# First attention of a two-block network: values' high and low parts in one tile, product by pairs of heads, halves added by VectorE

## What is computed

```python
dots  = einsum("bthd,bsd->bths", iq, ik)            # indexer
score = einsum("bth,bths->bts", iw, relu(dots))     # then causal
_, idx = lax.top_k(score, 256)                      # keys that a token may see
logits = einsum("bthd,btkd->bhtk", q, k_sel) * 64 ** -0.5 + bias
p = softmax(where(valid, logits, -inf))
o = einsum("bhtk,btkd->bthd", p, v_sel)
y_b = attn @ w_branch_b                             # merged with the convolution's y_a
```

## Time and profile before

| | |
|---|---|
| runs of the kernel | median 2590.57 us of 3 (2590.13 to 2590.76) |
| span of the profiled execution | 2590.4 us |
| PE busy | 2485.7 us (96%) |
| DVE, ACT, POOL busy | 1683.1, 950.8, 658.6 us |
| chain that ended last, by engine | PE 85%, DVE 8%, ACT 3% |
| the first attention's pipeline | about 497 to 650 us of the span |

### The profile page before, as it was taken

The page is one execution under the profiler, slowest core; times in us unless marked ns, Lnnn a source line. Parts: engine busy times, 40 slices in busy tenths (PEclk is TensorE's granted clock), DMA queues, the critical chain, the costliest instruction groups (busy, mean ns, idle before and its releaser), DMA issues.

```text
span 2590.4 us, 32111 instructions
## 1 busy us (share of the span) xinstructions
PE 2485.7 (96%) x12208; PEld 2054.2 (79%) x12208; DVE 1683.1 (65%) x2874; ACT 950.8 (37%) x1766; POOL 658.6 (25%) x536
## 2 busy tenths in 40 slices
PE   7899999988999999999999998999999999999998
PEld 5688888777787788888888886888877787888987
DVE  4599999477425898888654449585687556004843
ACT  5521212487224332222312144332333236226842
POOL 3157421576542100000000130000000035334753
PEclk9999999899999999999999999999999999999999
DMA  5112333100544365664533141323237223542242
GB/s 188 33 42 66 98 98 98 41 1 20 175 167 128 107 192 179 197 185 139 188 117 134 37 143 57 106 86 102 98 131 267 82 72 127 175 134 91 103 162 99
DMA packets 264324, 302.11 MB, mean 117 GB/s; under 512 B 11272, under 2 KB 216556, under 8 KB 264172
## 3 DMA queue, kind: packets, MB, share of 16 engines
q1 hardware_dynamic: 263860, 299.96, 35.6%
q10 hardware_dynamic: 312, 0.09, 0.0%
HBM read 228.15 MB, written 70.29 MB: 115 GB/s over the span
## 4 chain that ended last, share of the span: by engine, by line
PE 85%; DVE 8%; ACT 3%; issue 1%; DMA 1%; POOL 1%; SPq 0%; DVEq 0%; ACTq 0%; POOLq 0%
PE ps L67 82%; PE ps L70 3%; DVE sm L79 1%; DVE tmp L76 1%; ACT tmp L73 1%; ACT pth L73 1%; DVE pwa L76 1%; DVE wl L76 1%; DVE B2l L76 1%; DVE tmp L79 0%; DVE ptl L79 0%; DVE X L79 0%; ACT wh L73 0%; DVE pwb L76 0%; DVE XO L79 0%
## 5 line engine op out<-in xcount | busy, mean ns | idle before, releaser
L76 POOL TENSOR_TENSOR wl<-raw,wh 128x512 fp32r<-128x512 f32 (+1 forms) x224 | 294.4, 1335 | 1560.7 <-ACT wh L73 1560.6
L73 ACT ACTIVATE wh<-raw 128x512 fp32r<-128x512 f32 (+1 forms) x388 | 226.4, 621 | 238.1 <-PE ps L67 175.2
L67 PE MATMUL ps<-B2h,wh 128*128 128x512 f32 x616 | 243.0, 394 | 8.8 <-DVE tmp L76 7.7
L67 PE MATMUL ps<-B2l,wh 128*128 128x512 f32 x616 | 241.0, 391 | 0.0
L67 PE MATMUL ps<-B2h,wl 128*128 128x512 f32 x616 | 240.8, 391 | 0.0
L73 ACT ACTIVATE tmp<-ps 128x512 f32<-128x512 f32 (+5 forms) x161 | 116.9, 738 | 298.3 <-PE ps L67 283.9
L73 ACT ACTIVATE wh<-ws 128x512 fp32r<-128x512 f32 x152 | 94.4, 627 | 295.6 <-DVE ws L76 268.3
L67 PE MATMUL ps<-ah,wh 128*128 128x512 f32 (+1 forms) x608 | 193.0, 394 | 9.3 <-DVE al L76 5.1
L76 DVE TENSOR_TENSOR tmp<-tmp,ps 128x512 f32<-128x512 f32 x204 | 138.5, 684 | 84.9 <-PE ps L67 66.9
L67 PE MATMUL ps<-B3h,wh 128*128 128x512 f32 x448 | 178.3, 398 | 15.2 <-DVE B3l L76 7.0
L67 PE MATMUL ps<-al,wh 128*128 128x512 f32 (+1 forms) x608 | 190.9, 391 | 0.0
(11 more groups left out here) (295 smaller groups left out, 5767.2 us busy)
## 6 DMA issues: line engine op xcount, KB each, us to landing
ada<-in_ada_w SPq DMA_DIRECT2D x48, 512.0 KB, 3.6
raw<-in_w_in SPq DMA_DIRECT2D x37, 512.0 KB, 4.4
raw<-in_a_w_in SPq DMA_DIRECT2D x33, 512.0 KB, 4.7
gates<-tmp SPq DMA_DIRECT2D x32, 512.0 KB, 3.0
raw<-in_w_ffn_gate SPq DMA_DIRECT2D x24, 512.0 KB, 5.3
hd<-tmp SPq DMA_DIRECT2D x22, 512.0 KB, 4.2
gf<-hd SPq DMA_DIRECT2D x22, 512.0 KB, 7.2
raw<-in_a_w_out SPq DMA_DIRECT2D x20, 512.0 KB, 4.0
```

The costliest lines, as they stand in the source:

```text
L67: return self.e.matmul(*a, **k) if self.e else Ins()
L73: return self.e.activation(*a, **k) if self.e else Ins()
L76: return self.e.tensor_tensor(*a, **k) if self.e else Ins()
```

## The change

It puts the values' high part in columns 0 to 63 and the low part in columns 64 to 127 of one tile `VS`, without zeros. A product is made per pair of heads (n odd), with `VS` as stationary operand and two matmuls per tile of keys: by the high part of the weights and by the low part. The output's upper 64 partitions then hold the high values' product and the lower 64 the low values' product, for both heads (the product low by low, left out before, comes along). ACT copies the 256 columns to `OS`, and DVE adds the halves into `OT` with two instructions on 64 partitions. `stored` becomes the first stage on ACT, `folded` (new) the first on DVE, both with lag 7. The turned weights' buffers alternate by pairs: `pt1[n // 2 % 2]`, half n % 2. `VE`, `VO`, `VLE`, `VLO` and their zeroing on POOL go.

```diff
-        self.VE, self.VO, self.VLE, self.VLO = (m(f"vp{i}", i, FR) for i in range(4))
+        self.VS = m("vs", 0, FR)
+        self.OS = [m(f"os1{i}", 3, F32, 256, 1024 * i) for i in range(2)]
...
-        for n, v, h, l in self.value_pads(key, pads, row):
-            e.activation(h, v, ACT.Copy).then_inc(self.sig["ahi"].up(("vhi", key, n)), 1)
...
+        e.activation(hi, v, ACT.Copy).then_inc(self.sig["ahi"].up(("vhi", key)), 1)
...
         def values(n, part):
...
-            if n % 4 < 2:
+            if n % 2 == 0:
                 return
-            odd = hd % 2
-            if not odd and part == 0:
-                self.take(e, ("o", n // 4), ring=self.p_out)
-            po = self.ps(("o", n // 4))
-            V = (self.VO, self.VLO) if odd else (self.VE, self.VLE)
-            PH, PL = self.pt1[odd]
-            for event in (("zv1",), ("vlo", "v1", 1), ("pl", n - 2), ("pl", n)):
+            p = n // 2
+            if part == 0:
+                self.take(e, ("o", p), ring=self.p_out)
+            po = self.ps(("o", p))[:, 0:256]
+            PH, PL = self.pt1[p % 2]
+            for event in (("vlo", "v1"), ("pl", n - 1), ("pl", n)):
                 e.wait_ge(*self.at(*event))
             mid = (b + 2) // 2
             for i in (range(mid, b + 1) if part else range(mid)):
-                c, c2 = slice(i * 128, i * 128 + 128), slice(i * 256, i * 256 + 256)
-                ins = self.prods(e, po[:, 0:256], (V[0][:, c], V[1][:, c]), (PH[:, c2], PL[:, c2]),
-                                 odd == 0 and i == 0, odd == 1 and i == b)
+                V, c2 = self.VS[:, i * 128:i * 128 + 128], slice(i * 256, i * 256 + 256)
+                e.matmul(po, V, PH[:, c2], start=i == 0, stop=False)
+                ins = e.matmul(po, V, PL[:, c2], start=False, stop=i == b)
...
         def turned(n):
-            e.wait_ge(*(self.at("pv", self.pv(n - 4)) if n >= 4 else self.at(*self.PROJECTED)))
+            e.wait_ge(*(self.at("pv", n // 2 - 2) if n >= 4 else self.at(*self.PROJECTED)))
...
         def stored(n):
-            if n % 4 == 3:
...
+            if n % 2:
+                p = n // 2
+                e.wait_ge(*self.at("pv", p))
+                e.activation(self.OS[p % 2][:, :], self.ps(("o", p))[:, 0:256], ACT.Copy).then_inc(
+                    self.sig["evac"].up(("ocopy", p)), 1)
...
-        pipeline(64, [(4, turned), (2, norm), (7, stored), (0, exps), (4, conv)])
+        pipeline(64, [(7, stored), (4, turned), (2, norm), (0, exps), (4, conv)])
...
+        def folded(n):
+            if n % 2:
+                (b, hd), p = self.ITEMS1[n], n // 2
+                o = self.OT[:, hd // 2 * S + b * 128:hd // 2 * S + b * 128 + 128]
+                po, s = self.ps(("o", p)), self.OS[p % 2]
+                e.wait_ge(*self.at("ocopy", p))
+                e.tensor_tensor(o[0:64, :], po[64:128, 0:128], s[0:64, 0:128], ALU.add)
+                e.tensor_tensor(o[64:128, :], po[0:64, 128:256], s[64:128, 128:256], ALU.add).then_inc(
+                    vec.up(("ot", p), ("free", ("o", p))), 1)
...
-        pipeline(64, [(0, top_far), (2, norm), (0, top_near), (4, turned)])
+        pipeline(64, [(7, folded), (0, top_far), (2, norm), (0, top_near), (4, turned)])
...
-        self.pool_zero_v(e, ((self.VE, 64), (self.VLE, 64), (self.VO, 0), (self.VLO, 0)), ("zv1",),
-                         [self.half_projected()])
...
-    ATTENDED = (("pv", 31), ("ot", 15), ("pl", 63))
+    ATTENDED = (("pv", 31), ("ot", 31), ("pl", 63))
```

More of the change, by code:

```diff
@@ L1720, in pe_values_pads, with value_parts, act_values @@
         ins.then_inc(self.sig["prod"].up(("prod", key)), 1)
-    def value_pads(self, key, pads, row):
+    def value_parts(self, key, row):
         v = self.ps(key)[:, :].rearrange("p (i c) -> p i c", c=128)[:, :, row:row + 64]
-        for n, (H, L, c) in enumerate(((pads[0], pads[1], 0), (pads[2], pads[3], 64))):
-            yield n, v, *(x[:, :].rearrange("p (i c) -> p i c", c=128)[:, :, c:c + 64] for x in (H, L))
-    def act_value_pads(self, e, key, pads, row, after):
+        VS = self.VS[:, :].rearrange("p (i c) -> p i c", c=128)
+        return v, VS[:, :, 0:64], VS[:, :, 64:128]
+    def act_values(self, e, key, row, after):
+        v, hi, lo = self.value_parts(key, row)
         e.wait_ge(*self.at("prod", key))
@@ L1730, in act_value_pads, with dve_values @@
             e.wait_ge(*self.at(*event))
-        for n, v, h, l in self.value_pads(key, pads, row):
-            e.activation(h, v, ACT.Copy).then_inc(self.sig["ahi"].up(("vhi", key, n)), 1)
[L1734 to L1745, removed]
+        e.activation(hi, v, ACT.Copy).then_inc(self.sig["ahi"].up(("vhi", key)), 1)
+    def dve_values(self, e, key, row):
+        v, hi, lo = self.value_parts(key, row)
+        e.wait_ge(*self.at("vhi", key))
+        e.tensor_tensor(lo, v, hi.bitcast(F32), ALU.subtract).then_inc(
+            self.sig["vlo"].up(("vlo", key), ("free", key)), 1)
     def pe_attend(self, e):
@@ L1793, in values @@
             for i in (range(mid, b + 1) if part else range(mid)):
-                c, c2 = slice(i * 128, i * 128 + 128), slice(i * 256, i * 256 + 256)
-                ins = self.prods(e, po[:, 0:256], (V[0][:, c], V[1][:, c]), (PH[:, c2], PL[:, c2]),
-                                 odd == 0 and i == 0, odd == 1 and i == b)
+                V, c2 = self.VS[:, i * 128:i * 128 + 128], slice(i * 256, i * 256 + 256)
+                e.matmul(po, V, PH[:, c2], start=i == 0, stop=False)
+                ins = e.matmul(po, V, PL[:, c2], start=False, stop=i == b)
                 if i == b:
-                    ins.then_inc(self.sig["prod"].up(("pv", self.pv(n))), 1)
+                    ins.then_inc(self.sig["prod"].up(("pv", p)), 1)
         tiles = sorted(self.pool4, key=lambda i: max(x.taken for x in self.halves[2 * i:2 * i + 2]))
@@ L1819, in turns1 @@
         return [(0, 0, 4), (1, 4, b + 1)] if b > 3 else [(0, 0, b + 1)]
-    def pv(self, n):
-        return n // 4 * 2 + n % 2
     def last_of(self, i):
@@ L1843, in stored @@
         def stored(n):
-            b, hd = self.ITEMS1[n]
-            if n % 4 == 3:
[L1846 to L1850, removed]
+            if n % 2:
[3 more added lines that the diff above has]
+                    self.sig["evac"].up(("ocopy", p)), 1)
         def exps(n, late=True):
@@ L1875, in act_attend @@
                 norm(2 * n - 3, False)
-        self.act_value_pads(e, "v1", (self.VE, self.VLE, self.VO, self.VLO), 64, [self.half_projected()])
+        self.act_values(e, "v1", 64, [self.half_projected()])
         exps(4, False)
@@ L1889, in turned1 @@
         b, hd = self.ITEMS1[n]
-        PH, PL = (p[:, :].rearrange("p (i h c) -> p i h c", h=2, c=128)[:, :, n // 2 % 2, :] for p in self.pt1[n % 2])
+        PH, PL = (p[:, :].rearrange("p (i h c) -> p i h c", h=2, c=128)[:, :, n % 2, :] for p in self.pt1[n // 2 % 2])
         for part, i0, i1 in self.turns1(b):
@@ L1952, in dve_attend @@
         norm(3, False)
-        self.dve_value_pads(e, "v1", (self.VE, self.VLE, self.VO, self.VLO), 64)
+        self.dve_values(e, "v1", 64)
         for n in (4, 5):
```

## The result

The kernel after takes 2608.35 us (median of 4 runs, 2605.31 to 2608.76), the kernel before in the same job 2590.66 us: ratio 1.0061, interval 1.0049 to 1.0074. It is slower, as forecast, but by 17.7 us where the forecast said 6.4, and it lies above the range. Wherever the record has both, the time of a run lies 1.7 to 2.4 us above its span (2608.76 and 2606.8 for the profiled run of after; 2.2 to 2.4 us in runs of the kernel before), so the profiled execution of before would be one of about 2592.7 us (an estimate), 2 us above its median. A microsecond or two in a comparison of single stretches is therefore not sure.

A forecast was written before the change was run, and what follows sets the result against it. It took a ring of ACT's copy, DVE's fold and near part and ACT's exps to bound the changed kernel: body +6.4, transposes -2.8, tail +2.8, so +6.4 us, 2597.0 us; forecast 2594 to 2600, bounds together 2590 to 2604.

The forecast's parts named there:

- The ring: Attention body: copy, fold, far, near, exps, turned, norm, exps, next copy; sets the pace, 6.79 us per pair at b = 7.
- the table: Forecast ring times per block, four turns each: 6.79 us per pair at b = 7 down to 3.23 at b = 1.
- The price of the fold: DVE's two half-height adds per pair: 0.57 us without overlap, 0.40 kept for the range.
- Rival 1: The ring is cheap: fold at 0.40 us and unslowed DVE cl add give -0.3 us, no change; 22%.
- Body: +6.4 us: From the end of item 7's exps to item 63's: 141.0 us against 134.6 before.
- rival 3: PE's low clock lasts into b = 3; stalls add some 0.5 us in 12 pairs, 2603 us; 10%.
- Rival 4: Dearer ring: DVE's low part, far and near lie close, so jitter adds 2 to 4 us, 2600 us; 15%.
- To the last transposes: From the last exps to the last transposes: 5.6 us instead of 8.4, so -2.8 us.
- its cover is ample: Body, b = 7: PE has only 16 x 0.120 us of product per pair instead of 24, so isn't near the ring's pace.
- Behind the transposes: Tail: copies and fold +0.9 us, DVE's cl adds slowed beside POOL's (2.56 us each) +1.9; +2.8 us in all.
- the last product itself: After the attention: last values' product, three times shorter, lies beside the last convolution tile's load and gives nothing.
- Rival 2: Faster: the removed product ended last, not the ring; DVE's own sum, 6.0 us per pair at b = 7, gives 2575; 10%.

The follow-up runs named there:

- copy_early: Kernel after with ACT's copy of a pair's product one step earlier (lag 6), ahead of the exps instead of behind them; 2580.47 us, ratio 0.9962.
- third_mm: Kernel after with the matmul by the weights' high part issued twice per tile of keys, 144 matmuls more; 2612.08 us, ratio 1.0081.
- conv_last: Kernel after with the convolution's copies (ch) moved behind the last attention copy on ACT; 2599.40 us, ratio 1.0031.
- copy_early_conv: copy_early with the convolution's copies also moved behind the last attention copy, as in conv_last; 2578.41 us, ratio 0.9956.
- one_step_fold8: Kernel after with both parts of the values' product in one PE step (lag 6) and DVE's fold one step later (lag 8); 2611.47 us, ratio 1.0077.
- before_conv: Kernel before with the convolution's copies behind its last attention copy; 2592.02 us, ratio 1.0007.
- ring_on_before: Kernel before with an idle ACT copy and idle pair of half-height DVE adds, 28 times, where the change puts them; 2629.13 us, ratio 1.0150.
- work_on_before: ring_on_before with DVE's added adds one step later, so they don't wait for the copy; 2607.13 us, ratio 1.0065.

## Why the prediction was right and wrong

**The ring: right.** The 6.79 us per pair at b = 7 are 6.86 in the chain, the new waits of DVE (22.7 us in 28 stops up to 645) and of ACT (1.35 to 1.46 us per pair at b = 7) are those named, ACT's wait for the product is gone, the products are 144 and 144, and blocks 4 to 7 come out within 0.5 us of the table. One new wait wasn't named, PE's for the fold. copy_early, which differs from after by the copy's place alone, takes 19.4 us out of the body. "The time round this ring is a floor for the pace, whatever PE does" is third_mm's finding for blocks 3 to 7.

**The price of the fold: right, a little low.** The group on the tile `os`, 490 to 670, after (durations minimum/median/maximum in ns, first and last start):

```profile
L76 DVE TENSOR_TENSOR ot<-ps,os x64: 283/288/294, 500.7 to 665.7; 64x128 f32<-64x128 f32 x64
L73 ACT ACTIVATE os<-ps x32: 361/372/383, 500.3 to 665.0; 128x256 f32<-128x256 f32 x32
```

Each add takes 0.288 us, the two together 0.59, and the far part starts 0.62 us after the first (624.58 to 625.20); I had 0.57. There is no overlap at all. Rival 1 (0.40) is out. The Trainium skill (VectorE: DVE Perf Modes, "Two Vector instructions with no wait between them") has a rule by which an instruction that starts in another quadrant than the one before is held until that has finished. The trace agrees with it.

**The size of the body: term mis-sized.** "Body: +6.4 us" is +10.1. In blocks 4 to 7 the ring is 0.1 us per pair longer than summed, 1.8 us in all for 16 pairs. In the turn shown, fold, far and near take 0.10 more than summed, ACT's part 0.08 more (631.13 - 626.87 = 4.26 for 4.18), and the copy 0.11 less. The other 1.8 us are in blocks 1 to 3, 0.9 of it in b = 2. There the clock is low for longer (mean 0.66 over 490 to 520 against 0.77 before, 0.83 over 520 to 540 against 1.00), which was rival 3; its price of "some 0.5 us in 12 pairs", 6 us in all, was far too high. That the clock is the cause of these 1.8 us is argued from the rows, no run separates it. Rival 4 had the size of the excess (2 to 4 us) by jitter of DVE's own ring; the excess is evenly spread over blocks 4 to 7 (0.5, 0.5, 0.4, 0.4), which speaks for the ring's terms and against jitter.

**To the last transposes: step failed.** "5.6 us. -2.8 us" measures 652.91 - 645.08 = 7.8 us, so -0.6. My sum ran through ACT and DVE only. In the chain PE's product stands ahead of the transposes in the same step (646.03, 650.80: 1.22 and 1.23 us) and itself waits for the fold, for want of a second bank. I had written "its cover is ample" for PE in the body, which held, and used it where it didn't.

**Behind the transposes: step failed, and it is the largest.** "the last product itself, three times shorter there, lies beside that load and gives nothing." It doesn't lie there: it waits 7.52 us for the fold of pair 30, behind ACT's `ch` copies. "+2.8 us" measures (758.66 - 652.91) - (742.70 - 644.10) = +7.15. I had followed `stored` to its place at the head of ACT's list and counted two copies and the fold of delay, but hadn't asked what else waits for them; and the product's `take` of "o" was in the diff. conv_last takes 9.0 us back and so proves the place. Some 2 us of the stretch are the low clock at the head of the dense run, which was no term either. The two `cl` adds of DVE were sized well as a pair, 4.56 us against 5.1. But the 2.56 us for each was a mean read as a price. By themselves the two are, after:

```profile
L76 DVE TENSOR_TENSOR cl<-tmp,ch x2: 1226/2321/3416, 666.0 to 667.2; 128x1024 fp32r<-128x1024 f32 x2
```

```profile
667.19 3.42 DVE L76 TENSOR_TENSOR cl<-tmp,ch 128x1024 fp32r<-128x1024 f32 x1
```

```profile
666.15 3.37 POOL L76 TENSOR_TENSOR cl<-tmp,ch 128x1024 fp32r<-128x1024 f32 x1 [17.04 <-DVE ot L76]
```

The first add isn't slowed (1.23 us, as without POOL), and the second ends 1.1 us after POOL's first has ended (670.61 and 669.52).

Body +3.7, transposes +2.2 and tail +4.3 over the forecast, less the 0.67 gained ahead, are +9.5; the spans say 16.4 - 6.4 = +10.0.

**Rival 2 (faster, the ring isn't last): wrong for this kernel, right about the price.** It gave 6.0 us per pair when DVE's sum sets the pace, "2575" in all. With the ring cut, 24.3 us are measured for the four pairs of b = 7, 6.1 each, and 2580.47 us in all (2578.41 in copy_early_conv).

What stays open: a second place for "o". It would free PE's product from the fold, in the body and in one_step_fold8; it wasn't tried. Blocks 1 and 2 of before_conv are 3.0 us quicker than before's, with the clock at 0.94 over 490 to 520 instead of 0.77, though its change lies behind item 63; and its item 7 ends at 500.30, as early as after's. So up to 3 us in these two blocks, and the 0.67 us gained ahead, may be the single execution's: the body's loss is 10.1 us against before and 13.1 us against before_conv. Also open is why copy_early_conv's span is 14.4 us under before where the dense products end only 12.3 earlier.

## What to carry to other kernels

Where engines run a software pipeline in fixed order, ask of a new hand-over from A to B and back to A first what stands between its place and the next use on each queue. Here that cost more than the added instructions did (some 22 against 16.7 us on the kernel before). Sum the ring before placing it: here the same instructions give 2608 us with the copy behind the exps and 2580 with it ahead of them. And where a stage is moved to the head of a queue, follow it past the last item too: what it frees (here the one bank) may now come free behind a load that has nothing to do with it. A cut on an engine outside the ring brought little here (3.7 us of 17.3). Put it back in as an experiment; if the time stays, it was never the gain.

## What the runs showed of the hardware

- Two adds on 64 partitions each, whose inputs lie in other halves, start 0.31 us apart and last 0.288 each: no overlap. Two whole-height instructions of 128 columns (of another kind, the low parts) start 0.48 - 0.28 = 0.20 us apart. So the split by partitions took half as long again per instruction here as the columns alone, as far as two kinds of instruction compare.
- A wait can cost the clock too. ring_on_before and work_on_before do the same work and differ by one lag on DVE; from 520 to 640 the mean granted clock is 0.84 in the one and 0.97 in the other, and 1.00 in before and in copy_early_conv. Yet after is at 1.00 from 560 to 645, with PE busy 66.8 of 85 us. So I can say where the clock fell, not give a rule for it; a sum of durations misses it either way.
- DVE's and POOL's adds of 1024 columns from SBUF take turns in this trace. Two of DVE's without POOL take 2.36 us together (658.84 in conv_last). Beside POOL, DVE's first runs 666.05 to 667.28, POOL's first ends at 669.52, DVE's second at 670.61, POOL's second at 672.84, so each ends 1.1 us (DVE) or 2.2 us (POOL) after the other engine's. The durations of 3.4 us that the profile shows are then waits and work together, and a mean over them is no price of one add.
